# Softmax reciprocals by logarithm, exponential and a Newton step, a weight chunk's low part written over the chunk, and a new order of mixer steps, in a two-layer transformer kernel

## What is computed

```python
def mixer_block(h, ...):
    proj = rms_norm(h, norm1_g) @ w_in        # fq fk fv ff cq ckv krope sq sk sv gates
    log_decay = cumsum(log_sigmoid(ff + fox_forget_b))
    out_a = causal_block_attention(rms_norm(fq), rms_norm(fk), fv, log_decay)
    out_b = causal_block_attention(q, k, v_mla)          # from cq, ckv, rope
    out_c = sliding_window_attention(rms_norm(sq), rms_norm(sk), sv, sinks, slopes)
    g = sigmoid(gates)
    y = einsum('blnc,ncd->blnd', branches, w_branch)
    return h + sum(g * y) @ w_o

def conv_ffn(h, ...):
    u = rms_norm(h, norm2_g) @ w_up
    gate, val = split(conv3(u) + conv_b)
    return h + (silu(gate) * val) @ w_down
```

## Time and profile before

| | us |
|---|---|
| median of 3 runs | 2064.24 (2064.09 to 2067.81) |
| the profiled execution, its own time | 2067.04 |
| its span, first to last instruction | 2065.2 |
| PE busy | 1979.7 (96%) |
| DVE busy | 1144.9 (55%) |
| POOL busy | 1023.8 (50%) |
| ACT busy | 767.6 (37%) |
| mean granted clock of PE | 0.988 |

### The profile page before, as it was taken

How to read it: one execution, slowest core, us unless ns; L and a number is a source line. 1 busy time by engine, 2 the same in 40 slices (tenths; PEclk the granted TensorE clock), 3 DMA queues, 4 the chain that set the end, 5 groups by cost and what they waited for, 6 DMA issues and landing times.

```text
span 2065.2 us, 37779 instructions
## 1 busy us (share of the span) xinstructions
PE 1979.7 (96%) x15080; PEld 1879.0 (91%) x15080; DVE 1144.9 (55%) x2137; ACT 767.6 (37%) x1483; POOL 1023.8 (50%) x1306
## 2 busy tenths in 40 slices
PE   7899999899999999999998999999999999999999
PEld 7788997888999999999998889878889999999999
DVE  5665466676455665652356645656674656656411
ACT  4455566545222222220034555654452232222100
POOL 6755544443444444455476554543434445454543
PEclk9999999999999999999999999999999999999999
DMA  4112111111233323333332112111112323333332
GB/s 152 54 51 63 52 54 51 52 51 43 62 104 93 93 83 95 90 89 97 92 114 63 44 61 62 52 45 49 52 41 63 121 77 101 93 92 93 103 93 92
DMA packets 44803, 156.35 MB, mean 76 GB/s; under 512 B 5010, under 2 KB 5266, under 8 KB 44628
## 3 DMA queue, kind: packets, MB, share of 16 engines
q1 hardware_dynamic: 44484, 153.71, 24.6%
q10 hardware_dynamic: 144, 0.22, 0.0%
HBM read 149.58 MB, written 4.26 MB: 74 GB/s over the span
## 4 chain that ended last, share of the span: by engine, by line
PE 78%; DVE 11%; ACT 6%; issue 3%; DMA 0%; POOL 0%; ACTq 0%; DVEq 0%; SPq 0%
PE ps L1294 22%; PE ps L1297 21%; PE ps L1299 21%; PE ps L1528 5%; PE ps L1304 3%; DVE osum L1906 2%; DVE rstd L1619 1%; PE ps L1474 1%; PE ps L1435 1%; DVE ps L1876 1%; ACT xq L970 1%; DVE square L1614 1%; ACT square L987 1%; DVE q L1801 1%; ACT rstd L988 1%
## 5 line engine op out<-in xcount | busy, mean ns | idle before, releaser
L789 POOL TENSOR_TENSOR wl<-raw,wh 128x256 fp32r<-128x256 f32 x1080 | 800.6, 772 | 738.1 <-DVE wh L1598 729.9
L1294 PE MATMUL ps<-xh,wh 128*128 128x264 f32 (+1 forms) x2880 | 813.6, 304 | 5.8 <-POOL wl L789 2.7
L1297 PE MATMUL ps<-xl,wh 128*128 128x264 f32 (+1 forms) x2880 | 763.6, 285 | 0.0
L1299 PE MATMUL ps<-xh,wl 128*128 128x264 f32 (+1 forms) x2880 | 584.4, 284 | 0.0
L1294 PEld LDWEIGHTS ps<-xh,wh 128*128 128x128 f32 x2880 | 546.2, 190 | 32.7 <-issue 16.6
L1297 PEld LDWEIGHTS ps<-xl,wh 128*128 128x128 f32 x2880 | 546.5, 190 | 16.2 <-issue 7.2
L1299 PEld LDWEIGHTS ps<-xh,wl 128*128 128x128 f32 x2880 | 450.8, 190 | 0.0
L1598 DVE CAST wh<-raw 128x1024 fp32r<-128x1024 f32 x270 | 202.5, 750 | 166.1 <-PE ps L1294 152.2
L1898 DVE TENSOR_TENSOR ps<-ps,cst 128x128 f32<-128x128 f32 (+6 forms) x240 | 70.6, 296 | 209.7 <-PE ps L1480 139.6
L1297 PE MATMUL ps<-al,wh 128*128 128x264 f32 (+1 forms) x704 | 185.0, 283 | 0.0
L1294 PE MATMUL ps<-ah,wh 128*128 128x264 f32 (+1 forms) x704 | 183.6, 283 | 0.0
(11 more groups left out here) (183 smaller groups left out, 3208.1 us busy)
## 6 DMA issues: line engine op xcount, KB each, us to landing
raw<-weights SPq DMA_DIRECT2D x270, 512.0 KB, 3.6
h<-tokens SPq DMA_DIRECT2D x4, 528.0 KB, 6.5
h<-tokens SPq DMA_DIRECT2D x8, 264.0 KB, 5.3
residual<-h SPq DMA_DIRECT2D x8, 264.0 KB, 4.9
h<-residual SPq DMA_DIRECT2D x8, 264.0 KB, 5.9
out<-h SPq DMA_DIRECT2D x8, 256.0 KB, 4.7
cst<-constants SPq DMA_DIRECT2D x1, 1008.0 KB
extra<-positions SPq DMA_DIRECT2D x17, 4.1 KB
```

Of the source, the lines that this page charges most:

```text
L789: ins = nc.gpsimd.tensor_tensor(wl[c % SPLIT][:, part], raw[:, c % RAW, part], wh[c % SPLIT][:, part].bitcast(F32), ALU.subtract)
L1294: a = nc.tensor.matmul(out, a_hi, x_hi[:, sl], start=first, stop=False)
L1297: nc.tensor.matmul(out, a_hi, x_lo[:, sl], start=False, stop=False)
L1299: ins = nc.tensor.matmul(out, a_lo, x_hi[:, sl], start=False, stop=last)
```

## The change

1. **The reciprocal.** A new step "inverse" on ACT, right behind the second O of a job, computes exp(-ln(osum)) into a new tile `inverse` (two ACTIVATEs of 128x528). DVE's "recip" is now two passes over 128x528 (osum times inverse; then (that minus 2) times inverse), and "heads" multiplies `oraw` by -1 and by the result: a Newton step with its sign turned. The four quarters of L1906 are gone.
2. **The low part.** `wl` now has the same memory as `raw`, and POOL writes it over the chunk as loaded. `RAW` goes from 2 to 4, so that there are four buffers that serve as raw and as low part in turn, where there were two and three. A load into a buffer therefore waits until PE has begun the chunk after the one that was there (`s_start`), and is issued with the first block of the chunk that is three before it, where it was four.
3. **The order.** Other tables `ORDER`, `BEGIN`, `START`, `LAG`, `FIRST_LEAD` and `FIRST_STEP`.

```diff
-RAW, SPLIT = 2, 3
+RAW, SPLIT = 4, 3
...
-BEGIN = [65, 93, 121, 156, 192, 222, 250, 280, 318, 354, 391, 435]
+BEGIN = [65, 93, 122, 156, 194, 222, 250, 282, 318, 357, 391, 436]
...
-FIRST_LEAD, FIRST_STEP = 19, 1.0
-START = [16, 17, 16, 24, 30, 31, 2]
+FIRST_LEAD, FIRST_STEP = 16, 0.8
+START = [15, 17, 19, 22, 29, 33, 5]
...
-        for q in range(4):
-            put(i + q, 6, "recip", j, q)
+        put(i - 2, 6, "inverse", j)
+        put(i, 6, "recip", j, 0)
+        put(i + 1, 6, "recip", j, 1)
         if j >= OT_RING:
             i = max(i, end_of["y", (JOBS[j - OT_RING][0], KD - 1)] - 3)
-        put(i + 4, 2, "heads", j)
-        put(i + 4, 8, "head copy", j)
+        put(i + 2, 6, "heads", j)
+        put(i + 2, 8, "head copy", j)
...
+    raw_at = at[0]
     raw = sb("raw", [P, RAW, CW])
+    wl = sb("wl", [P, RAW, CW], F32R, offset=raw_at)
...
-                    sp.wait_ge(s_lo, n - RAW + 1)
+                    sp.wait_ge(s_start, n - RAW + 2)
...
-                    load(n // BLK + AHEAD + RAW)
+                    load(n // BLK + RAW - 1)
...
-                    ins = nc.gpsimd.tensor_tensor(wl[c % SPLIT][:, part], raw[:, c % RAW, part],
+                    ins = nc.gpsimd.tensor_tensor(wl[:, c % RAW, part], raw[:, c % RAW, part],
...
+                    elif s[0] == "inverse":
+                        j = s[1]
+                        logarithms()
+                        act.wait_ge(heads_copied.sem, heads_copied.at(l, j, 1))
+                        act.wait_ge(meta_heads_copied.sem, meta_heads_copied.at(l, j))
+                        if j > 0:
+                            act.wait_ge(heads_ready.sem, heads_ready.at(l, j - 1))
+                        follows(nc.scalar.activation(inverse[:, :], osum[:, :], ACT.Ln))
+                        nc.scalar.activation(inverse[:, :], inverse[:, :], ACT.Exp, scale=-1.0).then_inc(
+                            inverse_guess.sem, inverse_guess.tick((l, j)))
...
-                        nc.vector.reciprocal(osum[:, a:a + T // 4], osum[:, a:a + T // 4]).then_inc(
-                            dve_step.sem, dve_step.tick((l, "recip", j, q)))
...
+                            nc.vector.tensor_tensor(osum[:, :], osum[:, :], inverse[:, :], ALU.mult).then_inc(
+                                dve_step.sem, dve_step.tick((l, "recip", j, 0)))
...
+                            nc.vector.scalar_tensor_tensor(out=osum[:, :], in0=osum[:, :], scalar=-2.0, in1=inverse[:, :],
+                                                           op0=ALU.add, op1=ALU.mult).then_inc(
+                                dve_step.sem, dve_step.tick((l, "recip", j, 1)))
...
-                        nc.vector.tensor_tensor(oraw[:, :], oraw[:, :], osum[:, :], ALU.mult).then_inc(
+                        nc.vector.scalar_tensor_tensor(out=oraw[:, :], in0=oraw[:, :], scalar=-1.0, in1=osum[:, :],
+                                                       op0=ALU.mult, op1=ALU.mult).then_inc(
```

More of the change, by code:

```diff
@@ L81 @@
 STAT_LAG, NORM_LAG = 2, 4
-BEGIN = [65, 93, 121, 156, 192, 222, 250, 280, 318, 354, 391, 435]
-ORDER = ("fk0 gF0 fv0 fq1 fk1 gF1 fk2 fq2 fv1 fk3 fv2 fq3 gF2 sq0 gF3 fv3 sk sv gF4 sq1 gF5 sq2 gF6 gF7 yF0 cq0 cq1 yF1 sq3 yF2 yF3 ckv yF4 mq0 yF5 mv0 yF6 mq1 yF7 mk0 gS0 gS1 mv1 mq2 gS2 gS3 mq3 yS0 mk1 yS1 gS4 mq4 gS5 mq5 yS2 yS3 mk2 gS6 mv2 gS7 yS4 mq6 yS5 mq7 yS6 mk3 gM2 mv3 gM5 gM4 yS7 gM0 gM6 gM1 gM3 gM7")
+BEGIN = [65, 93, 122, 156, 194, 222, 250, 282, 318, 357, 391, 436]
+ORDER = ("gF0 fk0 fv0 fk1 fq1 gF1 fk2 fq2 fv1 fk3 fv2 fq3 gF2 sq0 gF3 fv3 sk sv gF4 sq1 gF5 gF6 sq2 yF0 gF7 cq0 cq1 yF1 sq3 yF2 yF3 ckv yF4 mq0 yF5 mv0 yF6 mq1 yF7 mk0 gS0 gS1 mv1 mq2 gS2 gS3 mq3 yS0 mk1 gS4 mq4 yS1 gS5 mq5 yS2 yS3 mk2 gS6 mv2 gS7 yS4 mq6 yS5 mq7 yS6 mk3 gM2 mv3 gM1 gM0 gM5 gM4 yS7 gM6 gM7 gM3")
 M_LEAD, M_STEP, NT_LEAD = 25, 1.8, 4
@@ L86 @@
 ZEROS = 10
-FIRST_LEAD, FIRST_STEP = 19, 1.0
-START = [16, 17, 16, 24, 30, 31, 2]
-LAG = {("dve", "layer stat"): 1, ("dve", "M"): 1, ("dve", "MM"): 1, ("act", "O"): -1, ("pool", "high"): -1, ("act", "head copy"): 1, ("dve", "STM"): -1, ("dve", "decay2"): 1, ("act", "tanh"): 1, ("dve", "rope2"): -1, ("dve", "decay"): -1, ("pool", "extras2"): -1, ("dve", "rope"): -1}
+FIRST_LEAD, FIRST_STEP = 16, 0.8
+START = [15, 17, 19, 22, 29, 33, 5]
+LAG = {("dve", "layer stat"): 3, ("dve", "M"): 1, ("dve", "MM"): 1, ("act", "O"): -1, ("pool", "high"): -1, ("act", "head copy"): 1, ("dve", "decay2"): 3, ("act", "tanh"): 1, ("dve", "rope2"): -1, ("dve", "decay"): 1, ("dve", "turn"): 1, ("act", "decay"): -1, ("pool", "extras2"): -1, ("dve", "rope"): 2, ("act", "high"): 1, ("dve", "heads"): -1, ("dve", "square low"): -1}
 def constants():
@@ L388, in build @@
     xl = sb("xl", [P, KD, T], F32R)
+    raw_at = at[0]
     raw = sb("raw", [P, RAW, CW])
+    wl = sb("wl", [P, RAW, CW], F32R, offset=raw_at)
     wh = [sb(f"wh{i}", [P, CW], F32R) for i in range(SPLIT)]
-    wl = [sb(f"wl{i}", [P, CW], F32R) for i in range(SPLIT)]
     h_at = at[0]
@@ L443, in build @@
     hsum = sb("hsum", [P, T])
+    inverse = sb("inverse", [P, T])
     cg = sb("cg", [P, 2, T], offset=late_at)
@@ L558, in build @@
     heads_ready = S("heads_ready")
+    inverse_guess = S("inverse_guess")
     heads_high = S("heads_high_part")
@@ L723, in _ @@
             sp.dma_start(extra[0:2, :], POS[0, :, :]).then_inc(s_cst, 16)
-            for n in range(2, AHEAD + RAW):
+            for n in range(2, RAW - 1):
                 load(n)
@@ L1286, in weights @@
                 a = n % BLK * P
-                return wh[c % SPLIT][:, a:a + P], wl[c % SPLIT][:, a:a + P]
+                return wh[c % SPLIT][:, a:a + P], wl[:, c % RAW, a:a + P]
             def gemm(n, slot, x_hi, x_lo, first, last, skip=0):
```

12 lines of the change are left out of this document (6 added, 6 removed).

## The result

The changed kernel takes 2077.45 us in the median of 8 runs (2073.27 to 2079.58), the kernel before 2065.3 (2063.96 to 2070.09): ratio 1.0054, 95% interval 1.0042 to 1.0066.

A forecast was written before the change was run, and what follows sets the result against it. PE was taken as the bound, busy 1979.7 of 2065.2 us, with short mixer waits behind other engines' queues. 2067.0 - 17.2 (waits) - 7 (clock) + 8 (inverses) = 2050.8; 2048 for the median, range 2030 to 2068.

The forecast's parts named there:

- The waits: PE's waits in the mixer, summed over the places: -8.6 us a layer, -17.2 for both.
- The clock: Four falls of PE's granted clock, by the value tile and 316 in each layer, 3.7 us each; half go: -7.
- Value tile: PE's 4.44 us wait before the first value tile falls to 2.1 as ACT's decay comes earlier: -2.3 a layer.
- The two waits that follow: Waits of 1.27 and 1.37 us after the value tile, from DVE and ACT being late there; half goes: -1.3.
- Job 0's end: PE's 2.81 us wait for job 1's shift: inverse delays the chain 1.3, shorter passes give back 0.7: +0.6.
- Meta scores at 315.10: A 0.92 us wait with meta exponentials behind high copies on ACT, which LAG puts a block later: -0.9.
- The others: Per layer: 306.43 -0.7, 357.94 -0.9, 363.38 -0.7, 387.61 -0.7, 429 to 455 -2.0, 500.81 +0.3 us.
- The passes' price: DVE's three new reciprocal passes at mean prices: 2.55 us a job for 4.57 before, 2.0 less, 24 times.
- Buffers: Loads issued a chunk later may delay casts by a microsecond, covered by PE two chunks behind: 0, up to +3.
- What I couldn't see: 24 inverses on ACT may delay what PE needs; one in four puts 1.3 us on the path: +8.
- The inverse chain: Rival, chance 0.12: ACT's queue of O copies, Ln, Exp, copy and square becomes the path, 16 inverses: 2076.

The follow-up runs named there:

- e17: The changed kernel without the lags of heads on DVE and of high on ACT: 2067.9 us, ratio 1.0006.
- e10: e9 with ORDER and BEGIN as in the changed kernel, LAG, START and FIRST_LEAD old: 2066.1 us, ratio 1.0014.
- e9: The kernel before with new reciprocal and buffers, old tables, job 0's decay transfers ten blocks later in SP's list: 2066.2 us, ratio 0.9999.
- e7: The changed kernel with the rope steps 8 blocks later (START 29, 33 now 37, 41): 2078.3 us, ratio 1.0051 to the kernel before.
- e13: e9 with heads one block earlier on DVE: 2077.7 us, ratio 1.0057 to the kernel before.
- e14: e9 with high one block later on ACT: 2076.9 us in the median of six, ratio 1.0053 to the kernel before.
- e12: The kernel before with 38 and 24 useless PE transposes in the waits for the value tile and job 1's shift: 2066.3 us, ratio 1.0008.
- e1: The kernel before with only the buffers changed (RAW 4, wl on raw, loads waiting on s_start): 2082.7 us, ratio 1.0080.
- e5: The kernel before with 14 and 9 useless PE transposes in the waits for the value tile and job 1's shift: 2070.3 us.
- e16: The kernel before with new reciprocal and buffers, plus the changed START, FIRST_LEAD, FIRST_STEP and lags of decay, rope, layer statistic: 2063.4 us, ratio 0.9990.

## Why the prediction was wrong, step by step

**In short.** Two steps failed. The waits, -17.2 with +8 for the inverses, so -9.2 in all, measured +2.3 of idle time in the profile. The clock, -7, measured +8.0 of busy time. The 12 us above the kernel before come from two lags, that of heads, which the prediction priced as part of a +0.6, and that of high, which it priced as a gain of 0.9. The 17 us below it that were forecast besides did not come at all: without the two lags (e17) PE idles 83.1 us against 85.5 before and the time is that of before.

**Value tile.** The size was right: 4.44 to 1.81 us, -2.6 for -2.3. But it comes from ORDER and BEGIN alone (e10), whose time is that of the kernel before: 4.9 us less waiting at the two value tiles than in e9 made no kernel faster.

**The two waits that follow.** Wrong: 1.27 and 1.37 were to halve, and became 3.00 and 1.12. The prediction took them for echoes of the first wait. By e7 I take them for DVE's own sum up to the job's shift, with the rope's passes slower beside POOL's `yk` (DVE's timeline of the changed kernel, against 0.49 each before):

```profile
61.34 1.24 DVE L1847 TENSOR_SCALAR gq<-cst,gain 128x528 f32<-128x528 f32 x1
62.50 1.56 DVE L1848 TENSOR_SCALAR gsb<-cst,gain 128x528 f32<-128x528 f32 x1
```

**Job 0's end.** The sign was right, the size was not, and it was the main step: +0.6 forecast, 2.81 to 3.85 measured, and 2.6 us more of slower work right behind it. The section on the change says that the three passes now stand ahead of the statistic; the prediction then priced only the inverse's 1.3 us against one pass. e13 shows that this placement by itself costs the whole kernel 11.5 us. DVE's statistic starts a chain through ACT's guess, the Newton step and the norm to PE's shift; with a pass of 1.71 us in front of it the shift came 1.5 us later. That is the way to the 6.8 us of waits in e13; the rest is time at the lower clock, which the forecast had only shrink. The prediction had said that the places count and not the sums, and then gave this place a mean price.

**Meta scores at 315.10.** Wrong in sign: high a block later was to give 0.9, and gave 0.1 there and cost elsewhere (e14, 11 us alone); with high moved, job 5 has the new wait of 0.92 at 283.94 in the changed kernel. The prediction looked at the wait that the lag had been in front of, and not at what stands behind it a block later.

**The others.** 306.43: -0.2 for -0.7. 357.94: -0.6 for -0.9. 363.38: gone, as forecast. 387.61: +0.5 for -0.7 (e10 and e13 have these 2.0 us too). 429 to 455 (now 438 to 464): 2.88 to 1.21, which looks like -1.7 for -2.0, but job 9's shift (453.49, a wait of 0.64) now comes at 466.53 with 1.28 and has only left the stretch; up to it PE loses 2.49, so -0.4. DVE is still busy 22.62 of 26 us. 500.81: 3.32 to 3.33.

**The passes' price.** 2.84 a job in place of 2.55. It depends on POOL: of 24 passes of L1930, the 10 that began while a POOL instruction ran took 1.56 us in the mean (1.12 to 1.74), the 14 that met none 0.71; of L1924, 8 took 1.48, and the 14 that met none 0.71; of L1920, 8 took 1.00 (0.70 to 1.58), and two of these were not slowed. The 62 quarters of the old reciprocal that met POOL took 959 ns in the mean, the 34 others 955. The rule of the Trainium skill, "SBUF — State Buffer", section "SBUF: two separate sides", that a DVE operation with two SBUF inputs and a GpSimd operation that reads SBUF exclude each other, agrees with the slowed passes, and with the one-input quarters, which never met it. The passes `gq` and `gsb` above read one tensor and were slowed all the same. The forecast spread its price evenly over the jobs; job 0's last two passes pay it in both layers, where POOL makes the low parts of the keys, and more than half of all passes pay nothing. The prediction held the mean of L1911 (741 ns) against the rule; only 6 of those 24 passes began beside POOL (0.77 to 0.99 us).

**The clock.** Wrong: -7 forecast, and PE's busy time rose by 8.0. The prediction looked for falls to go at the waits that shrink. Taking away those at the value tile gives next to nothing (e12), since DVE sets the pace there; the new falls behind job 1's shift and job 5's meta scores stand where PE has work, and cost: 2.6 us at the first, and at the second PE goes from the meta scores to the second head's scores in 12.2 us (283.94 to 296.12) in place of 9.0 (277.56 to 286.55). All executions together say the same: the span times (1 - mean clock), an estimate of what the lower clock can take, is 23.0 us in the mean for the kernel before (7 executions beside e1, and again 26 beside e5), 29.8 for the changed kernel (8) and 31.5 for e13 (6), against 23.3 for e9 (10). So about 7 of the 12 us are the clock's.

**Buffers.** 0 forecast and 0 in the changed kernel, where the cast waits 0.8 us for loads in all. But the reason given, PE's cover of two chunks, was not what holds: alone they cost 17 us (e1) through SP's queue, which the prediction named for spills and not for the decay rows. The changed tables bring the decay forward and so mend it (SP's transfers at 56.49, not 59.56); e16, with the new START and SP's list not mended by hand, loses nothing.

**What I couldn't see** (+8 for 24 inverses). On the old tables the size was fair: squares wait 6.7 us more in e9, and the relief of DVE pays it back (4.6 and some smaller ones). In the changed kernel they wait 5.1 us where they waited 4.7, so there the term is near 0. The inverse chain, the rival with the right time, would have needed 21 us of it and is not the cause.

What stays open: why the lags cost 12 and 11 us on the old order, 19 with all the others, and 6 and 2 in the changed one, and why the clock falls behind one wait and not behind another of the same length. Within one kernel, too, time goes with the clock: of the changed kernel's eight executions, the two at a mean clock of 0.987 and 0.988 took 2073.9 and 2073.3 us, the two with the lowest clock, 0.984, 2079.0 and 2079.6. Against the kernel before at 0.987 (2069.2 to 2070.4 in the executions beside e1 and e5) about 4 us of the 12 remain at an equal clock. No kernel of this study is faster than the one before beyond its interval; e16 is nearest (0.9977 to 1.0003), and the reciprocal and the buffers gain nothing by themselves on the old tables (e9).
